# Moved remainders in two attention loops, and constant products put ahead of three waits of each mixer

## The reference

```python
y = _layernorm(conv(u_a * sigmoid(u_b)), ln_w, ln_b); branch_3 = silu(y)
x = x + (sum_i gate_i * (branch_i @ w_branch[i])) @ w_out
```

```python
o = attention(q, k, v).reshape(B, S, W) * silu(g)
x = x + o @ w_out
```

## Time and profile before

| | |
|---|---|
| median of 3 runs | 2008.08 us (2007.81 to 2009.65) |
| the profiled execution's own time | 2006.37 us |
| its span, first to last instruction | 2004.6 us |
| PE busy | 1923.2 us (96%) |
| PE weight loads busy | 1766.9 us (88%) |
| DVE busy | 1289.0 us (64%) |
| ACT busy | 928.4 us (46%) |
| POOL busy | 124.3 us (6%) |
| mean granted clock of TensorE | 0.991 of 2.4 GHz |

### The profile page before, as it was taken

How to read it: one execution, slowest core, us unless ns; L and a number is a source line. 1 busy time by engine, 2 the same in 40 slices (tenths; PEclk the granted TensorE clock), 3 DMA queues, 4 the chain that set the end, 5 groups by cost and what they waited for, 6 DMA issues and landing times.

```text
span 2004.6 us, 34247 instructions
## 1 busy us (share of the span) xinstructions
PE 1923.2 (96%) x14639; PEld 1766.9 (88%) x14639; DVE 1289.0 (64%) x1835; ACT 928.4 (46%) x1110; POOL 124.3 (6%) x82
## 2 busy tenths in 40 slices
PE   7899999999998999999999999999999999889998
PEld 7789999999998899988788888888899989789978
DVE  5985566555579647655455558888887557854563
ACT  4443344433443423434444346777655443444453
POOL 0000000000000000000101010101200001100023
PEclk9999999999999999999999999999999999999999
DMA  7321245555442213545455468999999766224420
GB/s 279 106 85 54 93 171 190 175 184 189 153 148 85 67 62 132 191 168 167 160 166 177 150 219 284 326 329 327 324 178 179 135 103 129 94 65 144 129 85 22
DMA packets 235016, 321.84 MB, mean 161 GB/s; under 512 B 6257, under 2 KB 173425, under 8 KB 234609
## 3 DMA queue, kind: packets, MB, share of 16 engines
q1 hardware_dynamic: 234112, 317.76, 51.9%
q10 hardware_dynamic: 752, 1.90, 0.3%
HBM read 317.01 MB, written 1.05 MB: 159 GB/s over the span
## 4 chain that ended last, share of the span: by engine, by line
PE 82%; DVE 11%; ACT 3%; issue 2%; DMA 0%; SPq 0%; DVEq 0%; ACTq 0%
PE b L363 81%; DVE s_arena L379 4%; DVE s_ring_lo L472 2%; ACT s_wh L388 2%; PE b L1884 1%; DVE s_roots L379 1%; ACT s_arena L388 1%; DVE s_arena L2223 1%; DVE s_arena L382 0%; DMA s_ring<-w_in 0%; DVE s_arena L2145 0%; DVE s_arena L1333 0%; DVE s_roots L401 0%; ACT s_arena L385 0%; DVE s_roots L382 0%
## 5 line engine op out<-in xcount | busy, mean ns | idle before, releaser
L472 DVE TENSOR_TENSOR s_ring_lo<-s_ring,s_wh 128x2048 fp32r<-128x2048 f32 (+3 forms) x307 | 647.7, 2112 | 382.0 <-ACT s_wh L388 381.0
L388 ACT ACTIVATE s_wh<-s_ring 128x2048 fp32r<-128x2048 f32 (+3 forms) x329 | 574.3, 1747 | 270.2 <-PE b L363 264.3
L363 PE MATMUL b<-s_Hh,s_wh 128*128 128x256 f32 x1832 | 535.6, 292 | 4.8 <-DVE s_Hl L564 2.2
L363 PE MATMUL b<-s_Hl,s_wh 128*128 128x256 f32 x1832 | 522.1, 285 | 0.0
L363 PE MATMUL b<-s_Hh,s_ring_lo 128*128 128x256 f32 x1832 | 521.8, 285 | 0.0
L363 PEld LDWEIGHTS b<-s_Hh,s_wh 128*128 128x128 f32 x1832 | 354.5, 193 | 15.6 <-issue 6.1
L363 PEld LDWEIGHTS b<-s_Hl,s_wh 128*128 128x128 f32 x1832 | 354.7, 194 | 0.6
L363 PEld LDWEIGHTS b<-s_Hh,s_ring_lo 128*128 128x128 f32 x1832 | 354.5, 193 | 0.0
L363 PE MATMUL b<-s_wh,s_arena_r 128*128 128x512 f32 (+1 forms) x964 | 305.5, 389 | 3.2 <-DVE s_arena_r L2065 2.6
L363 PE MATMUL b<-s_arena_r,s_wh 128*128 128x256 f32 x1184 | 217.9, 285 | 9.6 <-ACT s_arena_r L388 5.9
L363 PEld LDWEIGHTS b<-s_wh,s_arena_r 128*128 128x128 f32 x964 | 180.4, 188 | 41.5 <-DVE s_arena_r L2065 3.9
(11 more groups left out here) (180 smaller groups left out, 1948.9 us busy)
## 6 DMA issues: line engine op xcount, KB each, us to landing
s_ring<-moe_w SPq DMA_DIRECT2D x96, 1024.0 KB, 5.2
s_ring<-moe_w SPq DMA_DIRECT2D x48, 768.0 KB, 4.4
s_ring<-ffn_w SPq DMA_DIRECT2D x33, 1024.0 KB, 4.9
s_ring<-w_gate SPq DMA_DIRECT2D x32, 1024.0 KB, 5.1
s_ring<-even_w_in SPq DMA_DIRECT2D x32, 1024.0 KB, 12.0
s_ring<-w_in SPq DMA_DIRECT2D x26, 1024.0 KB, 5.1
s_ring<-odd_w_in SPq DMA_DIRECT2D x16, 1024.0 KB, 5.3
s_ring<-w_out SPq DMA_DIRECT2D x8, 1024.0 KB, 6.6
```

The costliest lines, as they stand in the source:

```text
L363: return e.matmul(out, l, r, start=start, stop=True, skip_group_check=True)
L388: return e.activation(out, x, ACT.Copy, scale=scale)
L472: e.tensor_tensor(l_, r_, h_.bitcast(F), SUB).then_inc(*up(engine, z % "lo", i))
```

## The change

Two things are changed.

1. In both mixers, `fill` is called at three places: 11 products into bank 0 before the first product of branch 3, behind the wait for the bank and ahead of the waits for the branch; 5 into bank 7 before the sums of the squared keys (the wait for ACT's "a tanh", which empties the bank, now stands ahead of them, and the wait for "kk squares" behind); 9 into bank 7 ahead of the wait for "bonus".
2. In `attend_dve` the call of `attend_rest` moves from the beginning of the first half of a step to its end, behind the row minima of case t and the "attended" product of case t-2. Both the even and the odd layer use it.

```diff
             for f in range(4):
                 need_bank(e, l, 14 + f)
+                if f == 0:
+                    fill(e, bank_of(14), 11)
                 last = branch(3, f, f, bank_of(14 + f))
...
-            e.wait_ge(*on("kk squares", l))
             e.wait_ge(*on("a tanh", l, 1))
+            fill(e, b7, 5)
+            e.wait_ge(*on("kk squares", l))
             sums(e, table(b7, 2), [rtmp[:, i, :] for i in range(2)]).then_inc(*up("PE", "kk sums", l))
...
             yield
+            fill(e, b7, 9)
             e.wait_ge(*on("bonus", l))
...
         def attend_dve(e, name, cases, z):
             for t in range(len(cases) + 2):
-                if t >= 3 and cases[t - 3].part is not None:
-                    attend_rest(e, name, cases[t - 3])
                 if t < len(cases):
...
                     stt(e, case.out, o, 0.5, case.gate, MUL, MUL).then_inc(*up("V", "attended", name, t - 2))
+                if t >= 3 and cases[t - 3].part is not None:
+                    attend_rest(e, name, cases[t - 3])
                 yield
```

More of the change, by code:

```diff
@@ L1104, in rwkv_pe @@
             yield
+            e.wait_ge(*on("a tanh", l, 1))
+            fill(e, b7, 5)
             e.wait_ge(*on("kk squares", l))
-            e.wait_ge(*on("a tanh", l, 1))
             sums(e, table(b7, 2), [rtmp[:, i, :] for i in range(2)]).then_inc(*up("PE", "kk sums", l))
```

## The result

| | before | after |
|---|---|---|
| median | 2008.42 us (5 runs, 2007.81 to 2009.65) | 1998.44 us (5 runs, 1996.52 to 1999.42) |
| ratio, 95% interval | | 0.9947, 0.9933 to 0.9962 |
| the profiled execution's own time | 2006.37 us | 1996.56 us |
| its span | 2004.6 us | 1994.8 us |
| mean granted clock | 0.991 | 0.995 |

The kernel is 10.0 us faster, by its interval 7.6 to 13.5. Forecast were 8.5 us less and 1999.6 us. In the changed kernel the code stands 2 or 4 lines lower: L2248 is L2252, L1291 is L1295, L1124 is L1128.

The account below looks back on a forecast made before the run. The chain of waits was taken to lie 82% on PE and 11% on DVE. Branch fills 2.80, low halves 4.12 and one clock fall 1.53 sum to 8.45 us, 2008.08 to 1999.6 us; range 1996.5 to 2005.3.

Parts of the forecast that it names:

- The fills' own cost: Both mixers: 0.22 us a fill, hidden in PE's waits at key sums, bonus sums and branch 3; cost 0.
- In the second they overrun by 2.0-1.09-0.15, some 0.8 us: Second mixer's bonus sums: nine fills outlast PE's 1.09 us wait, but a later 2.45 us wait covers it.
- What the branch fills give: Branch 3, both mixers: less idling keeps PE's clock up for tiles f=0 and 1, 1.46 and 1.34 us gained.
- The low halves: Odd layer, t=4 and t=6: moved past POOL's piece they take 0.69 instead of 2.75 us; 4.12 us gained.
- the even sharing: Alternative reading of DVE and POOL contention: low half takes 1.4 us, so only 0.7 us gained each time.
- The margin of 0.7 us: Odd layer, t=4: the moved low half starts at 1941.7, 0.7 us after POOL's piece has ended.
- Even layer and t=8: Moving the low half there gains 0 and costs 0; bound 0.69 us lost at each of the two places.
- The fall behind t=6: Odd layer: with PE's wait cut to 1.1 us, the clock drop after it goes; 1.53 us gained.
- The falls are elsewhere in most executions: Rival: clock drops lie at other places in most runs, only the DVE part counts; 2004.0 us, chance 0.15.
- More falls go than counted: Rival: shifted later work also removes two or three other clock drops of 1.5 us; 1996 us, chance 0.12.
- the moved low half does nothing: Rival: POOL's piece also comes later or another wait holds the key tile; 2005.3 us, chance 0.08.
- it meets POOL anew: Rival: the low half meets the start of a POOL piece at its new place; slower, 2010.4 us, chance 0.05.

Follow-up runs that it names:

- move_only: Kernel before with the low halves moved as in the change, but no fills: 2001.77 us, ratio 0.9964.
- branch_fill_only: Kernel before with only the eleven fills ahead of branch 3, low halves not moved: 2005.93 us, ratio 0.9987.
- fills_only: Kernel before with all three kinds of fills, low halves left where they were: 2005.27 us, ratio 0.9983.
- early_fills_only: Kernel before with only the five and nine fills ahead of key and bonus sums, low halves not moved: 2008.47 us, ratio 0.9998.
- pool_quarters: Kernel before with POOL's subtraction of each late odd-layer weight piece cut into four instructions, no fills or move: 2002.38 us, ratio 0.9965.
- move_even_only: Kernel before with the low half moved in the even layer only, no fills: 2009.12 us, ratio 0.9999.

## Why the prediction was right

**The fills' own cost.** 0.22 us a fill: 11 took 2.62 us with the last one's latency, and eleven more cost 2.46 us. Cost 0 at all three places held: 0.25, 0.56 and 0.47 us of idling are left. The step that failed is a small one, "In the second they overrun by 2.0-1.09-0.15, some 0.8 us". They did not: PE still idled 0.56 us behind them. The 1.09 us of the earlier trace rows was short because the products ahead of it ran at 0.50 from 588 us on, as this window of the kernel before shows:

```profile
588.20:591.60 3.40, 3.40 (x18) 3.40 (x17) 3.02 (x14) 2.06 (x2) 0.00 (x0) 0.50 0.43 152
```

With five fills at the key sums the clock stays up and the wait has its 2.57 us, as in the first mixer. (Where the clock fell in the first mixer too, in *move_only* and *branch_fill_only*, the same wait there is 1.08 and 1.31 us.) I had costed one edit against a row that another edit changes. It was worth nothing here, as the 2.45 us wait would have covered it.

**What the branch fills give.** Forecast 1.46+1.34=2.80 us; the traces show 1.47 and 1.35, the medians 2.7 (*branch_fill_only*) and 3.4 us (*fills_only*). That the shorter idling, and not the shift of later work, keeps the clock up is shown by the count, 0 of 16 against 9 of 10; *early_fills_only*, which has the same early fills as the changed kernel, has both falls. The 2.80 us are what two single falls cost, and the forecast had that as the upper end. The profile I read happened to hold no double one; by the mean of the ten the two places were worth 2x1.63=3.3 us.

**The low halves.** Forecast 4.12 us; the traces show 2.07+2.06. That POOL's long instruction was the cause is shown by *pool_quarters*, and the even sharing that the prediction also weighed (1.4 us for the low half) is refuted by the whole 2.75 us ending behind POOL's. The margin of 0.7 us behind POOL's piece is there, 0.72. Even layer and t=8: 0 and 0, the first by *move_even_only*, the second by the lead, which is 9.80 us at the scores behind t=6 and 9.8 at the end of the span.

**The fall behind t=6.** Forecast 1.53 us, shown 1.54; the waits of 1.1 us were forecast and came as 1.07. *move_only* gained 6.9 us by the medians against 5.65 forecast for these two terms, inside its interval (4.6 to 10.0). A part of it may be regular: the wait at t=4 is followed by a fall in most executions, not only the one at t=6, which in the profile I read was the only one. Eight falls in ten waits make 1.6 an execution, where I counted one; at 1.53 us each the term should have been some 2.4 us.

**How much of the fit is luck.** The mechanism of each term held. The number for the clock was read in one execution, where the falls at these places cost less than in the mean. With the counts above the sum would have been 3.3+4.1+2.4=9.8 us (an estimate), which is nearer to the measured 10.0 than the forecast 8.5.

**The rivals.** *The falls are elsewhere in most executions* (2004.0) is refuted for the places named. *More falls go than counted* holds in part, though not at other places as it said: by the counts above the named places give 0.5 us more in the mixers and 0.9 us more in the odd layer than the profiled execution had to give back. The 1.3 us elsewhere in the profiled pair are a balance of falls gone and new, at places that change from run to run. That the moved low half does nothing (2005.3) and that it meets POOL anew (2010.4) are refuted by its 0.68 us and PE's 1.07 us.

## What to carry to other kernels

When a VectorE instruction takes four times its usual duration, look at what GpSimd runs beside it: moving the instruction behind work that isn't held up, or cutting GpSimd's long instruction into short ones, gave the same 7 us here (the second with luck: a quarter was just ending). A wait of PE of some 3 us costs more than its length where it isn't filled, 1.3 to 1.5 us more for a fall of the clock, 2.3 for a double one; constant products that end before the wait does take that away for nothing, and cost one for one as soon as they outlast it. They are worth it only where PE, not DVE, sets the pace behind the wait.

## What had not been expected of the hardware

- A fall of the clock is not tied to its wait: behind one and the same 2.97 us of idling it came 9 times in 10, and of two waits of 3.13 to 3.15 us in an execution mostly both, sometimes one, had one. A cost read in one profile is a frequent cost, not a sure one.
- A fall can last twice as long, in four of nine cases behind branch 3: 5.39 or 5.40 us for the 24 products, where a single one made it 4.37 to 4.53 and none 3.04.
- Cutting POOL's instruction into four freed DVE almost wholly (0.72 us against 0.69 in the even layer), since the low half began 0.17 us before a quarter's end. It has a price for POOL: that piece took 5.50 us (1939.39 to 1944.89) instead of 4.62.
